# Router scores and row norms as small matrix products over tokens; rank tables of later experts made between expert products

## The reference, cut to what matters

```python
x = x + ga1 * out_l
h2_l = modulate(rmsnorm(x, g_norm2[i]), sh2, sc2)        # rmsnorm(x) * g * (1 + sc2) + sh2
...
aff = jax.nn.sigmoid(jnp.matmul(h, w_router))            # (tokens, 16)
sel = aff + b_router
group_score = lax.top_k(sel.reshape(-1, 4, 4), 2)[0].sum(-1)
g_idx = jnp.argmax(group_score, axis=-1)
_, top_idx = lax.top_k(jnp.where(in_group, sel, -jnp.inf), 2)
w_top = aff[top_idx] / sum(aff[top_idx])
for e in range(16):
    y = y + gates[:, e] * ((silu(h @ w_e_gate[e]) * (h @ w_e_up[e])) @ w_e_down[e])
```

## Time and profile before

| | us |
|---|---|
| median of 3 runs | 1580.38 |
| lowest, highest | 1578.91, 1583.32 |
| the profiled execution | 1580.55 |
| its span, from the first to the last instruction | 1578.7 |
| PE busy, share of the span | 1403.4, 89% |
| DVE busy, share | 789.6, 50% |
| ACT busy, share | 672.9, 43% |
| mean granted TensorE clock | 0.938 of full speed |

### The profile page before, as it was taken

How to read it: one execution, slowest core, us unless ns; L and a number is a source line. 1 busy time by engine, 2 the same in 40 slices (tenths; PEclk the granted TensorE clock), 3 DMA queues, 4 the chain that set the end, 5 groups by cost and what they waited for, 6 DMA issues and landing times.

```text
span 1578.7 us, 20838 instructions
## 1 busy us (share of the span) xinstructions
PE 1403.4 (89%) x7774; PEld 1023.9 (65%) x7774; DVE 789.6 (50%) x1268; ACT 672.9 (43%) x1098; POOL 98.4 (6%) x98
## 2 busy tenths in 40 slices
PE   5799899997998996899999964999999887998882
PEld 2577677885556874788888853998875774543330
DVE  1512235423775626899999957465349643000002
ACT  4432113333665315588888853542357540111001
POOL 2100000000000000011121111000000000101001
PEclk8799999998998997799999986999999997999996
DMA  8752564335872231799999964363240358999994
GB/s 285 276 187 94 187 235 125 94 94 175 266 258 75 89 111 70 257 382 384 385 375 371 376 234 145 120 218 116 94 147 1 137 188 310 413 415 416 414 414 170
DMA packets 129365, 359.35 MB, mean 228 GB/s; under 512 B 14569, under 2 KB 14890, under 8 KB 128642
## 3 DMA queue, kind: packets, MB, share of 16 engines
q1 hardware_dynamic: 117522, 323.20, 56.3%
q0 software_dynamic: 10896, 31.87, 5.4%
q10 hardware_dynamic: 864, 3.15, 0.5%
HBM read 345.57 MB, written 25.17 MB: 235 GB/s over the span
## 4 chain that ended last, share of the span: by engine, by line
PE 74%; DMA 14%; DVE 5%; ACT 3%; issue 2%; POOL 0%; SPq 0%; POOLq 0%; ACTq 0%; DVEq 0%
PE ps L544 18%; PE ps L546 18%; PE ps L545 18%; DMA ring<-in_w_e_gate 9%; PE ps L796 3%; PE ps L1084 3%; PE ps L887 3%; PE ps L910 2%; PE ps L814 2%; PE ps L1106 1%; DMA ring<-in_w_e_down 1%; PE ps L898 1%; DMA w_raw<-in_w_in 1%; DMA w_raw<-in_w_ada 1%; PE ps L1027 1%
## 5 line engine op out<-in xcount | busy, mean ns | idle before, releaser
L540 DVE TENSOR_TENSOR w_lo<-w_raw,w_hi 128x1024 fp32r<-128x1024 f32 x224 | 270.7, 1223 | 342.2 <-ACT w_hi L536 340.0
L536 ACT ACTIVATE w_hi<-w_raw 128x1024 fp32r<-128x1024 f32 x224 | 235.7, 1059 | 360.4 <-PE ps L546 268.6
L544 PE MATMUL ps<-h_hi,w_hi 128*128 128x512 f32 (+1 forms) x704 | 250.6, 356 | 16.6 <-DVE h_lo L1526 9.1
L545 PE MATMUL ps<-h_lo,w_hi 128*128 128x512 f32 (+1 forms) x704 | 248.1, 352 | 0.0
L546 PE MATMUL ps<-h_hi,w_lo 128*128 128x512 f32 (+1 forms) x704 | 248.1, 352 | 0.0
L544 PEld LDWEIGHTS ps<-h_hi,w_hi 128*128 128x128 f32 x704 | 134.9, 192 | 39.3 <-DVE h_lo L1526 9.9
L546 PEld LDWEIGHTS ps<-h_hi,w_lo 128*128 128x128 f32 x704 | 134.8, 191 | 18.8
L545 PEld LDWEIGHTS ps<-h_lo,w_hi 128*128 128x128 f32 x704 | 134.8, 191 | 18.6 <-issue 0.2
L1084 PE MATMUL ps<-ring,xT 128*64 128x256 f32 x1024 | 131.0, 392 | 17.2 <-DMA ring<-in_w_e_up 9.8
L1084 PEld LDWEIGHTS ps<-ring,xT 128*64 128x64 f32 x1024 | 68.9, 138 | 80.1 <-DMA ring<-in_w_e_up 24.4
L540 DVE TENSOR_TENSOR w_lo_more<-w_raw,w_hi_more 128x1024 fp32r<-128x1024 f32 x96 | 115.3, 1222 | 5.2
(11 more groups left out here) (257 smaller groups left out, 2318.9 us busy)
## 6 DMA issues: line engine op xcount, KB each, us to landing
w_raw<-in_w_ada SPq DMA_DIRECT2D x96, 512.0 KB, 4.9
w_raw<-in_w_e_gate SPq DMA_DIRECT2D x64, 512.0 KB, 5.3
w_raw<-in_w_e_up SPq DMA_DIRECT2D x64, 512.0 KB, 7.4
w_raw<-in_w_e_down SPq DMA_DIRECT2D x64, 512.0 KB, 6.4
ring<-in_w_e_gate SPq DMA_DIRECT2D x64, 512.0 KB, 15.5
ring<-in_w_e_up SPq DMA_DIRECT2D x64, 512.0 KB, 15.4
ring<-in_w_e_down SPq DMA_DIRECT2D x64, 512.0 KB, 15.5
w_raw<-in_w_in SPq DMA_DIRECT2D x56, 512.0 KB, 4.3
```

The source lines that it names most:

```text
L536: act.activation(whi(n), raw[:, slot(n), :, :], ACT.Copy).then_inc(hi_ready, 1)
L540: dve.tensor_tensor(wlo(n), raw[:, slot(n), :, :], whi(n).bitcast(F32), ALU.subtract).then_inc(lo_ready, 1)
L544: pe.matmul(acc, sh, mh, start=first, stop=False, skip_group_check=True)
L545: pe.matmul(acc, sh, ml, start=False, stop=False, skip_group_check=True)
```

## The change

1. The sums of squares and the router scores come from one routine, `token_sums`, at the two places where `norm_sum` stood. Both have tokens on the partitions of the result: the square (or `X` itself) is the stationary operand, 128 features by 128 tokens, and what moves is one column of ones, or 16 columns of router weights multiplied by the scale (`wrs`). The constant part of the score, shift times router weights, is added by 8 further products for each of the two streams (8 in layer 1, which has one), at the start of the first part.
2. The root and the reciprocal are taken on 4 columns (`std4`, `rstd`). DVE makes the scores from sums and `rstd` (`token_scores`), PE repeats `rstd` over the partitions by transposes into bank ("rb"), DVE copies it to `rinv`, and multiplies `X` by it, now into one of four buffers (`xn4`), all eight tiles ahead of `route`. The sigmoid is taken of the scores in `lg`; the products of line 980, the transposes of line 986 and the bank ("log") are gone.
3. PE turns `h2T` in two halves of features over all tokens (`turn_h2`), no longer token tile by token tile.
4. In layer 0, only group 0 of `ids` is made ahead of the experts. Group 1 is made between the two products of expert 0, group 2 ahead of the transposes of expert 1, group 3 between the products of expert 1; DVE's `pick` for them stands between its splits. Layer 1 makes all four as before.

```diff
+        def token_sums(i, ks):
+            key, o = (i, "n2"), KT * norms[f"n2_{i}"]
+            sums = bank(key)
+            if ks[0] == 0:
+                take_tile(pe, key)
...
+                for s, c_ in ((1, 96), (0, 112))[i:]:
+                    for k in range(KT):
+                        pe.matmul(sums[:, c_:c_ + NE], spread(mod[i][:, 24 + k, s:s + 1], [P, P]), wr[:, k, :], ...)
+            for k in ks:
+                pe.wait_ge(n_sq, o + k + 1)
+                for t in tiles[i]:
+                    tc = slice(t * P, (t + 1) * P)
+                    pe.matmul(sums[:, t:t + 1], sq[:, k % 2, tc], ones[:, 0:1], ...)
+                    m = pe.matmul(sums[:, NE * (t + 1):NE * (t + 2)], X[:, k, tc], wrs[:, k, int(t < 2), :], ...)
                 m.then_inc(n_squ if k < KT - 1 else tile_done, 1)
...
                 if (s, ch) == (("WO", 1), 3):
-                    norm_sum(f"n2_{i}", (i, "n2"), c0, range(4))
+                    token_sums(i, range(4))
...
-            norm_sum(f"n2_{i}", (i, "n2"), c0, range(4, KT))
...
-            for k in range(KT):
-                pe.wait_ge(n_hf, KT * (2 * i + 1) + k + 1)
-                m = pe.matmul(bank(key)[0:NE, c0:T], wr[:, k, :], h2T[:, k, c0:T], start=k == 0, stop=k == KT - 1)
-            m.then_inc(tile_done, 1)
-            wait_emptied(pe, key)
-            key = (i, "aff")
+            token_sums(i, range(4, KT))
+            wait_emptied(pe, (i, "n2"))
+            key = (i, "rb")
             take_tile(pe, key)
             for t in tiles[i]:
-                m = pe.transpose(bank(key)[:, NE * t:NE * t + NE], affT[0:NE, t * P:(t + 1) * P], ident[0:NE, 0:NE])
+                m = pe.transpose(bank(key)[:, t * P:(t + 1) * P], spread(rstd[:, t:t + 1], [P, P]), ident)
...
+            def later_ids(g):
+                if g >= 2:
+                    pe.wait_ge(ids_out, g - 1)
+                slot_ids(g, ps[:, 7, :]).then_inc(ids_done, 1)
...
-            for g in range(4):
+            for g in range(4 if i else 1):
...
                 for e in range(2):
                     turn_tokens(e, e)
                     into_hidden(nb + 8 * e, e, 0)
+                    later_ids(1 + 2 * e)
                     if e:
                         turn_hidden(0)
                     into_hidden(nb + 8 * e + 4, e, 1)
+                    if e == 0:
+                        later_ids(2)
...
-            norm_rms(f"n2_{i}", col0[i])
+            act.activation(std4[:, t0:], bank(key)[:, t0:4], ACT.Sqrt, ...).then_inc(n_std, 1)
+            warm(ACT.Sigmoid)
+            wait_emptied(act, key)
+            act.activation(aff[:, t0:, :], lg[:, t0:, :], ACT.Sigmoid).then_inc(aff_ready, 1)
...
+        def token_scores(i):
...
+            dve.wait_ge(n_std, i + 1)
+            link(dve.reciprocal(rstd[:, t0:], std4[:, t0:]))
+            link(dve.tensor_tensor(lg[:, t0:, :], sums[...], spread(rstd[...]), ALU.mult))
...
+            dve.tensor_tensor(groups, groups, spread(shift, [P, 2 - i, 2, NE]), ALU.add).then_inc(free_dve, 1)
+            wait_tile(dve, (i, "rb"))
+            dve.tensor_copy(rinv[:, c0:T], bank(key)[:, c0:T]).then_inc(free_dve, 1)
...
             if i == 0:
                 tokens_lo(0)
-                splits(nb + 4, 3)
+                splits(nb + 4, 2)
+                later_picks(1)
+                splits(nb + 6, 2)
                 places(i)
-                splits(nb + 7, 1)
+                later_ids(1)
+                later_picks(2)
                 splits(nb + 8, 4)
+                later_ids(2)
                 tokens_lo(1)
+                later_picks(3)
                 hidden(nb + 8, 0)
-                splits(nb + 12, 4)
+                splits(nb + 12, 2)
+                later_ids(3)
+                splits(nb + 14, 2)
```

More of the change, by code:

```diff
@@ L232, in build @@
     wr = small("wr", [P, KT, NE])
+    wrs = small("wrs", [P, KT, 2, NE])
+    std4 = small("std4", [P, 4])
+    rstd = small("rstd", [P, 4])
     brb = small("brb", [P, NE])
@@ L443, in build @@
                 add_tile((i, "yT", k), "dve")
[L447 removed]
     done_at, signals = {}, 0
[L449 removed]
+    for key in plan:
         i = key[0]
@@ L709, in _ @@
                     fetch(e)
-                wait_emptied(pool, (i, "ids", 3))
+                pool.wait_ge(ids_out, 3)
                 pool.wait_ge(rt_loc[i], 1)
@@ L1005, in _, with slot_ids @@
             m.then_inc(tile_done, 1)
-            for g in range(4):
-                key = (i, "ids", g)
-                take_tile(pe, key)
+            def slot_ids(g, acc):
                 pe.wait_ge(picked, 4 * i + g + 1)
@@ L1375, in _ @@
             norm_squares(f"n2_{i}", col0[i], lambda k: (i, "WO", k // 4, k % 4), range(4, KT))
-            norm_rms(f"n2_{i}", col0[i])
-            act.wait_ge(mod_b, 1)
-            norm_apply(f"n2_{i}", col0[i], lambda k, s: sc2[i][:, k, s:s + 1], lambda k, s: mod[i][:, 24 + k, s:s + 1], False)
[L1379 to L1384, removed]
+            t0, key = tiles[i][0], (i, "n2")
+            wait_tile(act, key)
+            act.activation(std4[:, t0:], bank(key)[:, t0:4], ACT.Sqrt, bias=epst[:, 0:1], scale=1.0 / D).then_inc(n_std, 1)
+            warm(ACT.Sigmoid)
+            wait_emptied(act, key)
+            act.activation(aff[:, t0:, :], lg[:, t0:, :], ACT.Sigmoid).then_inc(aff_ready, 1)
+            act.wait_ge(mod_b, i + 1)
+            norm_apply(f"n2_{i}", col0[i], lambda k, s: sc2[i][:, k, s:s + 1], lambda k, s: mod[i][:, 24 + k, s:s + 1], False)
+            for half in range(2):
+                for t in tiles[i]:
                     key = (i, "h2", t, half)
@@ L1584, in empty_step @@
                 if s[1] == 0:
+                    dve.wait_ge(small_in, 32)
+                    for st in range(2):
+                        ins = dve.tensor_tensor(wrs[:, :, st, :], wr[:, :, :], spread(sc2[i][:, :, st:st + 1], [P, KT, NE]), ALU.mult)
+                    link(ins)
                     dve.wait_ge(x_back[i], 16)
@@ L1707, in experts_tokens, with picks, slot_ids, later_picks @@
             iota = spread(cs(C_IOTA, cap).unsqueeze(1).unsqueeze(1), [P, nt, 4, cap])
[L1708 to L1720, removed]
+            def picks(g):
+                ex = slice(4 * g, 4 * g + 4)
+                dve.tensor_tensor(chosen[:, t0:, ex, :], spread(mrank[:, t0:, ex].unsqueeze(3), [P, nt, 4, cap]), iota,
+                                  ALU.is_equal).then_inc(picked, 1)
+            def slot_ids(g):
+                key = (i, "ids", g)
+                wait_tile(dve, key)
+                w = 2 if i else 4
+                dve.tensor_scalar(ids[:, w * g:w * g + w], bank(key)[:, 0:2 * w:2], float(FAR), None, ALU.add).then_inc(free_dve, 1)
+            picks(0)
+            if i == 0:
+                slot_ids(0)
+                for ch in range(4):
+                    split_lo(dve, exp0[i] + ch)
+                return
+            for g in range(4):
+                if g < 3:
+                    picks(g + 1)
+                slot_ids(g)
+        def later_picks(g):
+            iota = spread(cs(C_IOTA, P).unsqueeze(1).unsqueeze(1), [P, 4, 4, P])
+            ex = slice(4 * g, 4 * g + 4)
+            dve.tensor_tensor(pick[:, :, ex, :], spread(mrank[:, :, ex].unsqueeze(3), [P, 4, 4, P]), iota,
+                              ALU.is_equal).then_inc(picked, 1)
+        def later_ids(g):
+            dve.wait_ge(ids_done, g)
+            dve.tensor_scalar(ids[:, 4 * g:4 * g + 4], ps[:, 7, 0:8:2], float(FAR), None, ALU.add).then_inc(ids_out, 1)
         def places(i):
```

74 lines of the change are left out of this document (48 added, 26 removed).

## The result

The changed kernel took 1598.26 us (median of 4 runs, 1596.06 to 1605.93) against 1581.20 for the kernel before on the same chip, a ratio of 1.0117 with a 95% interval of 1.0079 to 1.0154: slower by 1.2%. In a second session five runs gave 1601.75 (1599.41 to 1606.96), 1.0130 [1.0108, 1.0151]. The prediction was 1600, range 1584 to 1608.

What follows compares the result with a forecast made beforehand. The prediction took a chain of waits, three quarters on PE, as the bound. Layer 0: 23.7 - 8.0 - 4.8 + 6.6 = +17.5; layer 1 +2.6; 1580.55 + 20.1 = 1600.6, predicted 1600, range 1584 to 1608.

Steps and rivals of the forecast that it cites:

- The clock falls within the sums: Layer 0's new sums: narrow products lose full clock after 3.3 us; first part 18.0 us, +14.8; sums together +23.7.
- last chunk: Layer 0, 24 wide products behind the first part of the sums: they begin at half clock, +1.9 us.
- second part: Layer 0, second part of the new sums: 64 records, 10.8 us against 3.8, +7.0.
- Root to routing: Last norm sum to DVE's choice of experts: 8.3 us instead of 16.3, gain 8.0; in layer 1 gain 5.6.
- slack of 2 us for the features: Layer 0: transfers of `h2T` end near 21.5, first `ids` come at 23.3, so the features stay hidden.
- The last sentence of that paragraph: Root to routing, layer 0: had routing stood ahead of the `xn` products, their 5.4 us would have gained too.
- First fetch: Layer 0, first `ids` to PE turning expert 0: 6.1 us instead of 10.9, gain 4.8.
- Start of the experts: Layer 0, transposes of expert 0 to the end of expert 1: 40.8 us instead of 34.2, +6.6; later experts only shift.
- Layer 1's sums: Layer 1: first part +5.0 us, 24 products of 256 columns at half clock +1.8, second part +1.4, sum +8.2.
- Rival A: The clock holds in the new sums: layer 0 +4.0 us, layer 1 -1.5, total 1583; chance 0.13.
- B: Faster: clock holds and later `ids` fit in PE's waits, so the experts' start costs nothing: 1576.5 us; chance 0.06.
- C: Worse: half clock from the first record, `places` holds ACT longer; 1612 us, half of that 1606; chance 0.14.

Runs made afterwards that it cites:

- widened kernel: Changed kernel with 128 moving columns of ones instead of 1, 192 shift columns instead of 16, squares' sums in their own bank: 1587.22 us, 1.0052 of the kernel before.
- mixed kernel: Changed kernel with the first part of the sums in pairs between wide products of WO's last three chunks, second part unchanged: 1591.68 us, 1.0063 of the kernel before.

## Why the prediction came out

The time was right, 1600 against 1598 and 1602, and so, in the main, was the account behind it, with these sizes:

- **The clock falls within the sums.** Right, and shown by the widened and the mixed kernel. It fell 5.8 us after the first part began, not after the 3.3 assumed, so that part cost +12.1 instead of +14.8; last chunk +1.4 (+1.9), second part +6.7 (+7.0). Together +20.2 against 23.7: the largest miss, and nearly all of it the moment of the fall. The moment is a matter of the run. In the six profiles in which the first part is this same block, the clock fell 3.2, 3.3, 3.6, 5.3, 5.8 and 5.8 us after it began, and the block took, in the same order, 17.6, 17.5, 17.2, 15.7, 15.3 and 15.3 us. So the 3.3 us, and the 18.0 for the block, would have been close in three of them. The 3.3 stands in no row: the row from 614.8 to 618.3 shows 3.5 us.
- **Root to routing** -7.9 against -8.0; in layer 1 -5.5 against -5.6. The small steps were priced from rows of equal shape, and that held. The slack of 2 us for the features was about 1.5, as said above. The last sentence of that paragraph failed, as told above.
- **First fetch** -4.4 against -4.8.
- **Start of the experts** +6.9 against +6.6, but this agreement is in part luck. The forecast counted up to the end of expert 1, that is to the transposes of expert 2. These come 39.2 us after those of expert 0 (681.3 less 642.1) where 40.8 were foreseen: +5.2 and not +6.6, about the three groups of 1.68 us (1.8 foreseen). The first product of expert 1 began 24.3 us after the transposes of expert 0 (666.4 less 642.1; 25.4 foreseen, 20.9 before). The other +1.7 came after that: expert 2, from its transposes to those of expert 3, took 19.8 us instead of 18.0, where the prediction let the later experts only shift. There DVE was behind by its three `pick`, and PE waited 1.2 us for `he_lo` and `xg_lo`. It goes with the later tables alone: expert 2 takes 19.7 to 19.8 us in the profiles of every kernel here that has them, and 18.0 in those of every kernel that has not. With the fetch, the fourth part was to lose 1.8 net, and lost 2.5 in the trace and 3.3 alone.
- **Layer 1's sums** +7.8 against +8.2.
- **Not foreseen**: -2.6 ahead of the change, which is the run, +1.1 between the layers and +1.5 behind the last `sel`, where half-clock stretches lie otherwise (950.5 for 27.3 us against 939.3 for 23.9; from 1308.9 for 30.7 against 1304.5 for 20.5). That these three cancel is luck. So the profiled execution is 16.6 us longer where 20.1 were forecast, and the difference is that of layer 0's sums; by the medians of the two sessions the change costs 17.1 and 20.0.

Rival A (the clock holds, 1583) is what the widened kernel makes true; it took 1587.2. Its two parts in layer 0 lasted 12.3 and 7.1 us, where the rival's 96 and 64 records at 0.11 are 10.6 and 7.1; the wider shift products are the difference (5.20 us for 32 records against 3.48). They account for 1.7 of the 4 us that the kernel lies above the rival; the rest was not followed up. Rivals B and C did not occur. Two references and two readings in the prediction are off: the 4.63 us of DVE's splits stand in the earlier trace rows, and the 0.69 us there is the time of an `xn` product of 128x512, taken for the copy of the same size; the copy took 0.70. The clock that came back "about 4 us" after wide products began came back 3.4 us after them by the rows quoted (601.2 to 604.6); in the changed kernel it took 4.1 (594.8 to 598.9), so the term came out. The last chunk at half clock throughout would be 24 x 0.20 = 4.8 us, not the 3.7 in the upper bound.

The Trainium skill ("TensorE: Matmul & The Clock Gate", section "What's actually happening") makes the gate follow how busy PE has been. Here PE and its loads were busy for 9.40 of 9.40 us at a clock of 0.50, and in the widened kernel for 11.60 of 11.60 at 1.00, so busy time as the profile shows it does not tell the two apart. The same page (section "LDWEIGHTS (loading the stationary operand)") gives a load the time in ns of its columns over 1.2, which is an estimate of 107 ns for 128 columns, and names no clock. Two records of line 837 took 0.24 us at the full clock, near that estimate, and 0.45 at half, twice as long.

## What to carry to other kernels

A sum over partitions that is turned around so that its result has tokens on the partitions has four loads of 128 columns for every one of before, and where PE is on the path it costs more than the columns that it saves: price it by its loads, at both levels of the clock. Here it was better to keep the wide side moving, to put the new products where PE waits anyway, and to turn the small result; that gave the early routing for 0.5 us on the path. Work that is taken off a wait and put between the products of a stretch where PE never waits is paid in full, and if it delays the engine that feeds these products (here DVE, by three `pick`), it is paid once more in waits. What heads a path with little to spare (here the features for the fetch) can't be put back for a shorter one.

## What the runs showed of the hardware

- Products with 1 and 16 moving columns, back to back for 15 to 17.6 us, lost the full clock 3.2 to 5.8 us into the run in six profiles. In the changed kernel it came back at 598.9, within products of 512 columns, 4.1 us after these began; after the second part it stayed at half until 626.2, while PE turned features with 128 moving columns (from 620.5 on). With 128 columns in place of the 1 (and 192 in place of the 16 of the shift) they kept it, and the 128 cost nothing: a pair of lines 838 and 840 of the widened kernel took 0.45 us, as a pair of lines 835 and 837 at full clock.
- Records of narrow products behind loads of 128 columns follow each other at about twice the distance at half clock (two of line 837 in 0.45 us against 0.24).
- A transfer of the features to memory took 2.8 to 4.0 us to land on this path, and the fetch behind it 5.0 to 7.9 us.
